# Six shared weight products of a mixture-of-experts loop cut from 160 to 128 tokens, with the tokens beyond 128 done in the two larger bodies

## The chip, the core and the metric

The kernel runs on one core of one Trainium2 chip. The metric is the device time of one execution in microseconds (us). Inputs, weights and output are float32.

## The reference, cut to what matters

The program is one decoder block over 1024 tokens of width 1024: a mixer (a short convolution and a recurrence over chunks) and then a mixture of experts, in which the change lies. Each token goes to 4 of 32 experts. For the tokens of one expert the reference computes

```python
h = xb @ gu_w[e] + gu_b[e]                      # 1024 -> 2048: gate and up, interleaved
x_glu = jnp.minimum(h[:, 0::2], SWIGLU_LIMIT)
x_lin = jnp.clip(h[:, 1::2], -SWIGLU_LIMIT, SWIGLU_LIMIT)
act = x_glu * jax.nn.sigmoid(SWIGLU_ALPHA * x_glu) * (x_lin + 1.0)
return act @ dn_w[e] + dn_b[e]                  # 1024 -> 1024
```

and adds each result, times its gate, into the row of its token. Which tokens an expert has is known only on the chip, so each expert's number of tokens is a value that the engines read and branch on.

## The kernel before, in words

**Order of the program.** TensorE runs the input projections, the recurrence, the output projection with the router, and then the expert loop. The expert loop is a loop on each engine over 33 turns; turn 0 only prepares expert 0. One turn of TensorE (`expert_pe`) consists of:

1. `down_half(n, 0)`: the first half of the down projection of expert n (8 products, 512 columns wide);
2. `transpose_tokens`: the transposes of the next expert's tokens;
3. `down_rest(n)` if expert n has more than 128 tokens (32 products with 32 columns of weights each), otherwise one small product;
4. `down_half(n, 1)`: the second half;
5. one of three copies of `gate_up` for the next expert, chosen by a branch on its size: 128, 144 or 160 tokens (`SIZES`);
6. `gate_up_end`, code that all three sizes share.

**The gate and up products.** `gate_up` has the weights as the stationary operand (128 by 128) and the tokens `xT` as the moving one (128, 144 or 160 wide). For each of 8 tiles f it makes 8 products for the gate half (k = 0) and 8 for the up half (k = 1), which accumulate over kt in PSUM: `ps[:, f % 2, 0:160]` for the gate, `ps[:, f % 2, 160:320]` for the up (`C` is 160). That would be 128 products; of the last eight (f = 7, k = 1) the body makes only kt = 0 and 1 (`SHARED = 6`), so that a body has 122. The remaining six, kt = 2 to 7, are in `gate_up_end` (L1856), which all sizes run and which is therefore 160 wide whatever the size.

**Who waits for them.** After each tile f the semaphore `s_gu` is raised (for the last tile by `gate_up_end`). VectorE and ScalarE then make the activation from the PSUM bank (`glu`, L1306 to L1313, always 160 wide) and write `actT[:, f, :]`. `down_half(n, 0)` waits before its first product for `actT` up to f = 6, and before its last for f = 7. The queue of SyncE (L506) reloads the weight slots: slot 3, which the six products read, is reloaded for the next expert once `s_gu` says that the last tile is done.

**Records.** A float32 product is seen in the trace as two weight loads (on PEld) and two matmul records (on PE): the 122 products of a body are 244 matmul records and 244 weight loads, the six products of L1856 are 12 and 12. The loop's code for TensorE is aligned to a block of 256 instructions (`pe.addr_align(FETCH_BLOCK, ...)`).

Of the kernel before, what the change touches and what calls it, by code (L numbers as in the profile page):

```python
# [13 lines left out]
P = 128  # L14
T = 1024
D = 1024
KT = D // P
# [12 lines left out]
C = 160  # L30
# [85 lines left out]
def build(nc, x, w_in_t, prm_d, lora_d, wgate_d, normw_d, w_out, router_w, router_b, gub_d, gu_w, dn_w,  # L116
          dn_b, consts_d, list0_d, entry_d, out, conv_d, bonus_d, xn_d, acc_d, list_d):
    ctx = ExitStack()
    with ctx:
# [8 lines left out]
        def at(kb, *shape):  # L128

            n = math.prod(shape)  # L130
            o = int(kb * 256)
            v = arena[:, o:o + n]
            if len(shape) == 2:
                v = v.rearrange("p (a b) -> p a b", b=shape[1])
            elif len(shape) == 3:
                v = v.rearrange("p (a b c) -> p a b c", b=shape[1], c=shape[2])
            elif len(shape) == 4:
                v = v.rearrange("p (a b c d) -> p a b c d", b=shape[1], c=shape[2], d=shape[3])
            return v

        ps = ctx.enter_context(nc.psum_tensor("ps", [P, 8, HALF], FP))
# [91 lines left out]
        wslot = [at(o, KT, HALF) for o in (0, 16, 32, 64, 80, 96)]  # L233
        xg = at(48, D)
        xg2 = at(52, PW)
        xT = at(136, KT, C)
# [106 lines left out]
        SHARED = 6  # L343
# [1060 lines left out]
        def _(pe):  # L1404
# [381 lines left out]
            for t in range(TT + 2):  # L1786
# [12 lines left out]
                if 0 <= u < TT:  # L1799
                    pe.wait_ge(s_xn2, u + 1)  # L1800
                    for g in range(2):
                        if u:
                            pe.wait_ge(s_t2c, 2 * u + g - 1)
                        for k in range(4):
                            kt = 4 * g + k
                            last = nc.tensor.transpose(ps[:, 4 + g, k * P:(k + 1) * P], xn2[u % 2][:, kt * P:(kt + 1) * P],
                                                       ident)
# [5 lines left out]
                if 0 <= u < TT:  # L1813
# [7 lines left out]
                    for kt in range(KT):  # L1821
                        g = kt % (P // E)
                        last = nc.tensor.matmul(ps[g * E:(g + 1) * E, 6, 0:P], rw[:, kt, :], xn2T[u % 2][:, kt, :],
                                                start=kt < P // E, stop=kt >= KT - P // E, skip_group_check=True)
# [9 lines left out]
            def gate_up(n, m, size):  # L1834

                for f in range(KT):
                    u = f // 2
                    if f % 2 == 0:
                        pe.wait_ge(s_wt[u], 16 * n + 16)
                    if f >= 2:  # L1840
                        pe.wait_ge(s_gd, 8 * n + KT + f - 1)
                    for k in range(2):
                        for kt in range(KT - SHARED if f == KT - 1 and k else KT):
                            if f == 0 and k == 0 and kt in (0, 4):
                                pe.wait_ge(s_xe, 3 * m + (2 if kt == 0 and size == P else 3))
                            o = (f % 2 * 2 + k) * P
                            last = nc.tensor.matmul(ps[:, f % 2, k * C:k * C + size],  # L1847
                                                    wslot[u][:, kt, o:o + P], xT[:, kt, 0:size],
                                                    start=kt == 0, stop=kt == KT - 1, skip_group_check=f == KT - 1)
                    if f < KT - 1:  # L1850
                        last.then_inc(s_gu, 1)

            def gate_up_end():

                for kt in range(KT - SHARED, KT):
                    last = nc.tensor.matmul(ps[:, 1, C:2 * C], wslot[3][:, kt, 3 * P:4 * P], xT[:, kt, :],  # L1856
                                            start=False, stop=kt == KT - 1, skip_group_check=True)
                last.then_inc(s_gu, 1)

# [35 lines left out]
            def expert_pe(r):  # L1895
# [4 lines left out]
                with pe.Fori(0, E + 1) as turn:  # L1900
                    n, m = r * E + turn - 1, r * (E + 1) + turn
                    with pe.If(turn > 0):
                        down_half(n, 0)
                    size = size_at(turn)
                    transpose_tokens(m)
                    with pe.If(size > 1):
                        down_rest(n)
                    with pe.If(size == 1):
                        pe.wait_ge(s_ye, 3 * n + 5)
                        nc.tensor.matmul(ps[0:REST, 6, 0:REST], actT[:, 0, P:C], ident[:, 0:REST], start=True, stop=True  # L1910
                                         ).then_inc(s_dn, 1)
                    with pe.If(turn > 0):
                        down_half(n, 1)
                    pe.wait_ge(s_sz, 2)
                    need = size_at(turn + 1)
                    with pe.If(need == 3):
                        gate_up(n + 1, m + 1, SIZES[2])
                    with pe.Else():
                        with pe.If(need == 2):
                            gate_up(n + 1, m + 1, SIZES[1])  # L1920
                        with pe.Else():
                            with pe.If(need == 1):
                                gate_up(n + 1, m + 1, SIZES[0])
                    with pe.If(need > 0):
                        gate_up_end()
# [62 lines left out]
```

## Time and profile before

| | |
|---|---|
| median of 3 runs | 2351.17 us (2351.09 to 2353.74) |
| profiled execution | 2356.62 us, its span 2355.1 us |
| mean granted TensorE clock | 0.99 |
| TensorE busy | 2296.2 us (98%) |
| weight loads busy | 1702.4 us (72%) |
| VectorE, ScalarE, GpSimd busy | 757.2, 483.4, 343.6 us |
| the chain that ended last, TensorE's share | 93% |

The profile has for each engine the records of its instructions, with start and duration. A matmul's record is longer than the time it takes from its neighbours, because matmuls overlap in the pipeline: what a record costs is the distance between starts, which the views give as the length of a stretch over its number of records. "The chain that ended last" is followed back from the last instruction, at each step to what released it or to the instruction before it on its engine; its pieces don't overlap, so a piece's length over its count is that distance. "issue" is time in which nothing that the profile shows was waited for.

### The profile page before, as it was taken

Reading aid. Unit: us, or ns where it says so; the run is one execution under the profiler, and the core shown is the slowest. Engines: PE = TensorE matmul, PEld = TensorE weight load, DVE = VectorE, ACT = ScalarE, POOL = GpSimd, SP = SyncE. Lnnn points to the kernel's source line nnn. Section 1 sums busy time; section 2 is a strip of 40 time slices with the busy share of each in tenths; the row PEclk is TensorE's granted clock in tenths of the full one; section 3 lists DMA queues with packets and bytes.
Section 4 is the critical chain, followed back from the end, with each engine's and each line's share of the span. In section 5 each row is a group of like instructions: output and inputs, shape, how many; then the busy total and the mean of one; then the engine's idle time right before and its main releaser. Section 6 shows DMA issues by size and latency. Waiting matters only on the chain.

```text
span 2355.1 us, 46545 instructions
## 1 busy us (share of the span) xinstructions
PE 2296.2 (98%) x18398; PEld 1702.4 (72%) x18399; DVE 757.2 (32%) x1802; ACT 483.4 (21%) x1008; POOL 343.6 (15%) x360
## 2 busy tenths in 40 slices
PE   7999999899999999999999999999999999999997
PEld 5443444799834578887888788877887788778876
DVE  2466511345333422322222222222222232222324
ACT  3323200244423301111111111111111111111113
POOL 0000000121102302111211121111111121112112
PEclk9999999999999899999999999999999999999998
DMA  3121111322352457986797779777797699768977
GB/s 120 36 70 36 49 59 62 93 76 71 105 239 100 142 223 279 335 349 263 295 339 308 282 276 337 286 303 300 295 348 305 254 335 353 285 245 326 346 305 256
DMA packets 111393, 534.97 MB, mean 227 GB/s; under 512 B 26755, under 2 KB 60695, under 8 KB 86736
## 3 DMA queue, kind: packets, MB, share of 16 engines
q1 hardware_dynamic: 89184, 489.30, 53.4%
q0 software_dynamic: 22160, 44.98, 7.6%
q8 instruction: 35, 0.57, 0.1%
q14 instruction: 14, 0.11, 0.0%
HBM read 485.24 MB, written 40.05 MB: 223 GB/s over the span
## 4 chain that ended last, share of the span: by engine, by line
PE 93%; DVE 3%; DMA 2%; issue 1%; ACT 1%; POOL 0%; SPq 0%; POOLq 0%; DVEq 0%; another core or an unknown queue 0%; ACTq 0%
PE ps L1847 38%; PE ps L1867 18%; PE ps L1409 13%; PE ps L1759 5%; PE ps L1877 2%; PE ps L1856 2%; PE ps L1554 2%; PE ps L1566 2%; PE ps L1560 1%; PE ps L1886 1%; DVE arena L1092 1%; PE ps L1440 1%; PE ps L1536 1%; DMA idx_g<-list_s 1%; PE ps L1655 0%
## 5 line engine op out<-in xcount | busy, mean ns | idle before, releaser
L1847 PEld LDWEIGHTS ps<-arena 128*128 128x128 f32 x7808 | 927.6, 191 | 17.5 <-issue 15.0
L1847 PE MATMUL ps<-arena 128*128 128x128 f32 (+2 forms) x7808 | 928.5, 282 | 2.3 <-ACT arena L937 2.3
L1867 PE MATMUL ps<-arena 128*128 128x512 f32 x1024 | 454.5, 597 | 0.0
L1409 PE MATMUL ps<-arena 128*128 128x512 f32 x832 | 361.1, 593 | 0.8 <-ACT arena L741 0.8
L1867 PEld LDWEIGHTS ps<-arena 128*128 128x128 f32 x1024 | 190.7, 190 | 222.1 <-issue 221.2
L1409 PEld LDWEIGHTS ps<-arena 128*128 128x128 f32 x832 | 157.2, 190 | 201.4 <-issue 201.4
L1306 DVE TENSOR_SCALAR arena<-ps,arena 128x160 f32<-128x160 f32 x256 | 98.3, 384 | 616.9 <-PE ps L1847 537.6
L942 ACT ACTIVATE arena<-arena 128x160 f32<-128x160 f32 x256 | 86.1, 336 | 825.2 <-DVE arena L1306 825.2
L644 POOL DMA_INDIRECT sum_s<-arena,idx_s x31 | 51.5, 1661 | 825.1 <-ACT arena L957 825.1
L1759 PE MATMUL ps<-arena 128*128 128x512 f32 x256 | 114.6, 602 | 1.5 <-DVE arena L1208 1.5
L1310 DVE SCALAR_TENSOR_TENSOR arena<-arena 128x160 f32<-128x160 f32 x256 | 83.3, 325 | 49.9 <-ACT arena L942 49.9
L1307 DVE TENSOR_SCALAR arena<-ps,arena 128x160 f32<-128x160 f32 x256 | 96.1, 376 | 0.0
L628 POOL DMA_INDIRECT arena<-xn_s,idx_g x33 | 36.5, 1105 | 391.9 <-issue 202.3
L1759 PEld LDWEIGHTS ps<-arena 128*128 128x128 f32 x256 | 48.3, 193 | 58.9 <-issue 58.9
L1327 DVE TENSOR_TENSOR arena<-ps,arena 128x512 f32<-128x512 f32 x31 | 21.4, 692 | 205.4 <-PE ps L1867 205.4
L1313 DVE TENSOR_TENSOR arena<-arena 128x160 f32<-128x160 f32 x256 | 83.3, 325 | 8.8
L934 ACT COPY arena<-ps 128x512 f32<-128x512 f32 x66 | 35.5, 588 | 213.2 <-PE ps L1886 212.0
L1323 DVE TENSOR_TENSOR arena<-ps,arena 128x512 f32<-128x512 f32 x31 | 21.4, 692 | 162.8 <-PE ps L1867 162.8
L957 ACT ACTIVATE arena<-arena,idx_s 128x512 f32<-128x512 f32 x31 | 22.4, 722 | 202.1 <-DVE arena L1327 202.1
L1856 PE MATMUL ps<-arena 128*128 128x160 f32 x384 | 58.1, 301 | 2.5 <-issue 2.5
L1856 PEld LDWEIGHTS ps<-arena 128*128 128x128 f32 x384 | 53.7, 191 | 2.7 <-issue 2.7
L1877 PE MATMUL ps<-arena 128*32 128x256 f32 x960 | 54.9, 380 | 0.0
(259 smaller groups left out, 1824.0 us busy)
## 6 DMA issues: line engine op xcount, KB each, us to landing
arena<-gu_w SPq DMA_DIRECT2D x128, 2048.0 KB, 13.4
arena<-dn_w SPq DMA_DIRECT2D x64, 2048.0 KB, 14.3
arena<-dn_b SPq DMA_DIRECT2D x32, 512.0 KB, 16.2
arena<-w_in_t SPq DMA_DIRECT2D x26, 512.0 KB, 3.2
arena<-arena SPq DMA_DIRECT2D x50, 256.0 KB, 2.7
arena<-x SPq DMA_DIRECT2D x4, 1024.0 KB, 8.3
arena<-w_out SPq DMA_DIRECT2D x2, 2048.0 KB, 10.7
arena<-x SPq DMA_DIRECT2D x8, 512.0 KB, 5.4
```

Source lines behind the costliest of these rows:

```text
L644: pool.indirect_dma_start(acc_d, bass.IndirectOffsetOnAxis(ap=idx_s[:, 0:1], axis=0), Yt, None, compute_op=ALU.add).then_inc(s_sc, 16)
L942: nc.scalar.activation(sgm[f % 2], gt[f % 2], ACT.Sigmoid, scale=ALPHA).then_inc(s_gs, 1)
L1306: nc.vector.tensor_scalar(gt[b], ps[:, b, 0:C], g0, LIMIT, ALU.add, ALU.min).then_inc(s_g1, 1)
L1307: nc.vector.tensor_scalar(lt[b], ps[:, b, C:2 * C], g1, LIMIT + 1, ALU.add, ALU.min).then_inc(s_gd, 1)
L1310: nc.vector.scalar_tensor_tensor(out=lt[b], in0=lt[b], scalar=1 - LIMIT, in1=sgm[b], op0=ALU.max, op1=ALU.mult).then_inc(s_l1, 1)
L1313: nc.vector.tensor_tensor(actT[:, f, :], lt[b], gt[b], ALU.mult).then_inc(s_act, 1)
L1409: last = nc.tensor.matmul(ps[:, bank + h, :], win[:, slot, kt * P:(kt + 1) * P], xnT[:, kt, h * HALF:(h + 1) * HALF], start=kt == 0, stop= ...
L1759: last = nc.tensor.matmul(ps[:, 2 * (t % 2) + h, :], mixT[:, k, t * P:(t + 1) * P], wo[:, k % RT, h * HALF:(h + 1) * HALF], start=k == 0, ...
L1847: last = nc.tensor.matmul(ps[:, f % 2, k * C:k * C + size], wslot[u][:, kt, o:o + P], xT[:, kt, 0:size], start=kt == 0, stop=kt == KT - 1, ...
L1856: last = nc.tensor.matmul(ps[:, 1, C:2 * C], wslot[3][:, kt, 3 * P:4 * P], xT[:, kt, :], start=False, stop=kt == KT - 1, skip_group_check= ...
L1867: last = nc.tensor.matmul(ps[:, 2 + h, :], actT[:, ft, 0:P], wslot[4 + h][:, ft, :], start=ft == 0, stop=ft == KT - 1)
L1877: last = nc.tensor.matmul(ps[g * REST:(g + 1) * REST, 6, 0:PW], actT[:, ft, P:C], wslot[4 + g // 2][:, ft, g % 2 * PW:(g % 2 + 1) * PW], s ...
```

## The change

The six products that all sizes share now cover 128 tokens (columns C to C + 128 of the bank), and each of the two larger bodies (144 and 160 tokens) ends with six products of its own, with the same stationary weights, over the 16 or 32 tokens beyond 128. `size` is a Python number, so that the 128-token body's code is unchanged. The same change is in the copy of the loop for further rounds, which isn't run with these inputs.

```diff
                     if f < KT - 1:
                         last.then_inc(s_gu, 1)
+                if size > P:
+                    for kt in range(KT - SHARED, KT):
+                        nc.tensor.matmul(ps[:, 1, C + P:C + size], wslot[3][:, kt, 3 * P:4 * P], xT[:, kt, P:size],
+                                         start=False, stop=kt == KT - 1, skip_group_check=True)
 
             def gate_up_end():
 
                 for kt in range(KT - SHARED, KT):
-                    last = nc.tensor.matmul(ps[:, 1, C:2 * C], wslot[3][:, kt, 3 * P:4 * P], xT[:, kt, :],
+                    last = nc.tensor.matmul(ps[:, 1, C:C + P], wslot[3][:, kt, 3 * P:4 * P], xT[:, kt, 0:P],
                                             start=False, stop=kt == KT - 1, skip_group_check=True)
                 last.then_inc(s_gu, 1)
```

## Rows read from the trace of the kernel before

**Rows 1.** The page: engines' busy time, and the chain's shares by line.
```profile
PE 2296.2 (98%) x18398; PEld 1702.4 (72%) x18399; DVE 757.2 (32%) x1802; ACT 483.4 (21%) x1008; POOL 343.6 (15%) x360
...
PE ps L1847 38%; PE ps L1867 18%; PE ps L1409 13%; PE ps L1759 5%; PE ps L1877 2%; PE ps L1856 2%; PE ps L1554 2%; PE ps L1566 2%; PE ps L1560 1%; PE ps L1886 1%; DVE arena L1092 1%; PE ps L1440 1%; PE ps L1536 1%; DMA idx_g<-list_s 1%; PE ps L1655 0%
```

**Rows 2.** Busy time of each engine in stretches of the expert loop.
```profile
core 0: us, PE busy (x) PEld busy (x) DVE busy (x) ACT busy (x) POOL busy (x), PEclk, DMA share, GB/s
...
822.00:857.00 35.00, 34.80 (x244) 34.80 (x244) 9.28 (x28) 3.79 (x9) 6.73 (x8) 0.95 0.89 338
...
860.00:869.00 9.00, 9.00 (x26) 5.07 (x26) 1.33 (x4) 0.34 (x1) 0.00 (x0) 0.81 0.63 231
...
935.00:2324.00 1389.00, 1389.00 (x9760) 1138.80 (x9759) 370.71 (x1044) 213.61 (x451) 242.73 (x240) 1.00 0.81 308
```

**Rows 3.** The chain that ended last: start, us, what; four stretches of it.
```profile
1450.68 33.14 PE ps L1847 x244
1483.83 1.63 PE ps L1856 x12
1485.46 6.87 PE ps L1867 x16
...
1504.07 29.89 PE ps L1847 x244
1533.96 1.63 PE ps L1856 x12
1535.59 6.87 PE ps L1867 x16
...
2069.34 29.89 PE ps L1847 x244
...
2119.47 27.24 PE ps L1847 x244
2146.71 1.63 PE ps L1856 x12
2148.35 6.87 PE ps L1867 x16
```

**Rows 4.** TensorE's groups by line and form: count, busy us, mean ns.
```profile
L1847 PE MATMUL ps<-arena 128*128 128x128 f32 x4148 | 466.2, 275 | 0.0
...
L1847 PE MATMUL ps<-arena 128*128 128x144 f32 x2928 | 360.6, 286 | 0.0
...
L1847 PE MATMUL ps<-arena 128*128 128x160 f32 x732 | 101.7, 302 | 2.3 <-ACT arena L937 2.3
L1856 PE MATMUL ps<-arena 128*128 128x160 f32 x384 | 58.1, 301 | 2.5 <-issue 2.5
```

**Rows 5.** Timeline of TensorE's matmuls in the token lists: start, us, line, form, count.
```profile
796.68 2.37 PE L1782 MATMUL ps<-cst,arena 128*128 128x1 f32 x20
```

**Rows 6.** The line L1782: duration of its records, min/median/max in ns.
```profile
L1782 PEld LDWEIGHTS ps<-cst,arena x32: 192/192/333, 796.7 to 809.9; 128*128 128x128 f32 x32
L1782 PE MATMUL ps<-cst,arena x32: 250/250/372, 796.7 to 810.0; 128*128 128x1 f32 x32
```

**Rows 7.** The chain in the router stage, with 32-wide products.
```profile
716.05 0.34 PE ps L1776 x2
716.39 0.22 PE ps L1777 x2
...
723.56 0.14 PE ps L1770 x2
```

**Rows 8.** The chain, turn 0 and the start of turn 1.
```profile
822.20 35.09 PE ps L1847 x244
857.29 2.46 issue
859.75 2.43 PE ps L1856 x12
862.17 8.02 PE ps L1867 x16
```

**Rows 9.** The DMA queues, 852 to 870 us: packets, MB, share of 16 engines.
```profile
q8 instruction: 2, 0.03, 0.7%
```

**Rows 10.** The DMA queues, 1000 to 2340 us: the whole list.
```profile
## 3 DMA queue, kind: packets, MB, share of 16 engines
q1 hardware_dynamic: 35155, 375.56, 70.1%
q0 software_dynamic: 17472, 33.80, 10.6%
issues: line engine op xcount, KB each, median us to landing
```

**Rows 11.** Timeline of VectorE and TensorE around L1856 in a 128-token turn.
```profile
2278.08 0.33 DVE L1313 TENSOR_TENSOR arena<-arena 128x160 f32<-128x160 f32 x1
2278.78 1.80 PE L1856 MATMUL ps<-arena 128*128 128x160 f32 x12
2280.41 4.03 PE L1867 MATMUL ps<-arena 128*128 128x512 f32 x9
...
2281.94 0.33 DVE L1313 TENSOR_TENSOR arena<-arena 128x160 f32<-128x160 f32 x1
```

**Rows 12.** Waits of SyncE's queue, 880 to 2290 us.
```profile
SPq L506 <- PE ps L1856: 217.2, 30, 8.2
```

**Rows 13.** The chain at its end.
```profile
2288.72 7.08 PE ps L1867 x16
2295.82 0.70 DVE arena L1327
...
2301.72 12.42 DMA idx_g<-list_s
```

## The prediction

> **What bounds the kernel now.** I read the page first: TensorE is busy for 98% of the span, and lines of TensorE make up 93% of the chain that ended last, the gate and up bodies (L1847) alone 38% and the shared end L1856 2% [rows 1]. A share of busy time can mislead, so I then read the stretches of the expert loop: from 935 to 2324 us TensorE was busy for all of 1389.00 us, at a granted clock of 1.00 (2.4 GHz), while VectorE, ScalarE and GpSimd had 371, 214 and 243 us and the DMA engines 0.81 of the time [rows 2]. Last the chain itself: in a turn of each size, body, shared end and down projection follow each other with no gap (1483.83 + 1.63 = 1485.46, and so in the others) [rows 3]. So in the loop nothing counts but the distance between the starts of TensorE's records. Whatever a product costs there is paid in full, and whatever is saved is gained in full.
>
> **What sets that distance.** A body is 244 matmul records. The reader is to divide each body's length by 244 [rows 3]: 33.14 us is 135.8 ns a record at 160 wide, 29.89 us is 122.5 ns at 144, 27.24 us is 111.6 ns at 128. From 160 to 144 the distance falls by 13.3 ns, which is two cycles of 2.4 GHz for each of the 16 columns (32 / 2.4 = 13.3); from 144 to 128 it falls by only 10.9. At 128 wide something else has begun to bind. What it is can be read off products that have hardly any columns: L1782 has 128 by 128 stationary operands, each loaded anew, and a moving operand one column wide. Twenty of its records lie in 2.37 us [rows 5]; less the last one's 250 ns [rows 6] that leaves 2.12 us for 19 distances, 111.6 ns each. That is the distance of the 128-wide records to the digit, with 1 column in place of 128. So the load of the next weights sets a floor of 111.6 ns a record, and at 128 columns or fewer the columns are free. The narrowing therefore gains only the part above the floor, and a product of 16 or 32 columns costs as much as one of 128.
>
> **The sizes.** By form there are 4148, 2928 and 732 records of 128, 144 and 160 wide [rows 4]; over 244 these are 17, 12 and 3 experts, 32 in all. L1856 has 384 records, 12 for each expert, as it should.
>
> **Part 1, the shared end, 160 to 128 wide.** Twelve records take 1.63 us now (135.8 ns each) [rows 3], and 12 x 111.6 = 1.34 us after: 0.29 us less for each expert. Two of the 32 need a word. The last expert's end lies behind the point at which the chain leaves TensorE for the last time (2295.82 us) [rows 13]; it counts for nothing. The first one's end comes after a wait of 2.46 us for instructions, with a clock that is granted at 0.81 on average in that stretch [rows 2, 8]; it took 2.43 us, and in proportion to its columns would fall by 0.49. Against this, the records queued ahead of that wait will be shorter (below), so that I count it at 0.29 as well. 31 x 0.29 = 9.0 us less.
>
> **Part 2, six products more in the larger bodies.** Six products are 12 records with a weight load each, which all lie on TensorE's path since nothing else does. 12 x 111.6 ns = 1.34 us, for 12 + 3 = 15 experts: 20.1 us more. All 15 lie before the chain leaves TensorE; the last body 144 wide starts at 2069.34 [rows 3]. The trace has no 16-wide product with these weights, so this price must be bounded. Above: a record 16 or 32 wide can't well cost more than one 144 wide in the same place, 122.5 ns, or 22.1 us in all. Below: records with 32 moving columns in the router stage stand in the chain as two in 0.22 us, two in 0.34 and two in 0.14 [rows 7]. The last is 70 ns each, but only because the first of the two has its weights loaded behind a 512-wide record; 0.22 us, in the midst of narrow ones, is 110 ns. In the new place the record before the first narrow one is 144 or 160 wide, and hides no more of a load than it does now. 70 ns would be 12.6 us in all. I take 111.6, the row of twenty in sequence, which is nearest in everything but the width (1 where 16 and 32 are wanted, and 128 gives the same).
>
> There is a rule that speaks for a much lower price. The Trainium skill, in "TensorEngine Tiling (Array Packing)", section Performance Considerations, says that a matmul has some 60 cycles of overhead and that one of a single column takes as long as one of 60. By it alone the twelve records would be 12 x 60 / 2.4 = 300 ns, an estimate from that page, and the change would gain 4.5 us (180 records at 25 ns, less 9.0). "TensorE: Matmul & The Clock Gate", section LDWEIGHTS, gives a weight load 128 columns over 1.2 GHz, 107 ns, and there the trace agrees nearly (111.6 measured).
>
> **Part 3, the rest, at nothing.** The shared end is now over 0.29 us sooner after the body of a 128-token expert. `down_half` waits for the activation of tile 6 before its first product: VectorE ends it at 2278.41, and L1867 starts at 2280.41 [rows 11], so 2.0 us of cover become 1.7. The activation of tile 7 ends at 2282.27, 1.9 us after that start, and its product is the last of eight that take 6.87 us: 4 us of cover stay. If the first cover were gone, each 0.1 us missing would cost 17 x 0.1 = 1.7 us. In the larger bodies both covers grow. SyncE's queue stands at L506 and waits for L1856 in 30 turns, 217.2 us in all [rows 12]: it waits for TensorE and not the other way. Weight slot 3 is asked for 1.05 us later in the larger turns and 0.29 earlier in the small ones, and with the DMA engines at 0.81 no transfer comes to limit TensorE. VectorE reads the same 160 columns as before.
>
> **The sum.** -9.0 + 20.1 = +11.1 us. A 128-token turn becomes 0.29 us shorter, a larger one 1.05 us longer. Against the profiled execution, 2356.62 us with a span of 2355.1, this gives 2367.7. That execution was 5.4 us above the median of the runs (2351.17); the same 11.1 us on the median gives 2362.3 us, 0.47% more.
>
> **The rivals.** About 0.2%, 4.7 us, is what a measurement of this kernel can tell from no change.
>
> *A. Narrow products are nearly free.* If a record of 16 or 32 columns cost its columns or a small fixed time, and its weight load lay hidden, the change would be faster. The point from which the sign turns is where 180 records cost the 9.0 us saved: 50 ns a record. At 25 ns it is 4.5 - 9.0 = -4.5, or 2346.7 us; at nothing, 2342.2 us. Against it are the twenty records of L1782 [rows 5], which have the least columns possible and yet stand 111.6 ns apart. For it is only the 0.14 us for two behind a wide record [rows 7]; at that 70 ns the sum is 12.6 - 9.0 = +3.6, 2354.8 us, within the band, as is all between 24 and 76 ns.
>
> *B. The code no longer stays on the chip.* The larger bodies get 24 instructions each, 12 loads and 12 matmuls. The cost of a jump to code that isn't there is in the trace: 2.46 us in turn 0, then L1856 at 2.43 in place of 1.63 and L1867 at 8.02 in place of 6.87 at the lower clock, 4.4 us together [rows 3, 8], with two transfers of instructions near it [rows 9]; from 1000 to 2340 us the list of queues has none [rows 10]. So all that the loop runs stays resident. If the 48 instructions ended that, with one such stall in each turn with a larger body, it would be 15 x 4.4 = 66 us: about 2428 us. Per turn's distinct code I count from the records 3 x 488 for the bodies, 24 for the shared end, 64 + 128 for the down projection, 24 for the transposes and the small product: 1704, and 1752 after, without waits and branches. "Runtime: NRT & Kernel Launch", section Instruction fetch mechanics, gives TensorE room for 2048 instructions; by that page the loop fits before and after.
>
> *C. The one stall shifts.* The code behind the larger bodies moves by 24 and 48 instructions. The wait of turn 0 may vanish (-4.4: 2357.9 us), or one more may show in the first turns (+4.4: 2366.7 us). The records ahead of the jump become shorter as well, 12 x 24 ns = 0.3 us less cover, so that a small lengthening is likelier than not; it is in the 0.2 us that I gave up in part 1.
>
> *D. The change does nothing to the pace of the shared end*, because 128-wide products there stay at 135.8. The bodies of 128 tokens, with the same weights' form, speak against it. It would be +20.1, 2371.3 us.
>
> **How the numbers follow.** The forecast, 2362.3 with its own range from 2360.5 to 2364 (a price of 107 to 116 ns for a narrow record gives -0.8 and +0.8, the rest is the scatter of a median), has 0.80. C has 0.09, on both sides alike. B has 0.03, D 0.02. A has 0.01 below 24 ns and 0.05 in the band. The range takes in the forecast and C: 2357.5 to 2367. Faster by over 0.2% is A's first part, 0.01; within the band A's second, 0.05; slower 0.94.
>
> **What would show it.** Right: L1847's records 16 wide (144 in number) and 32 wide (36) in the larger bodies, each six products 1.34 us in the chain; L1856 128 wide with 1.34 us for 12 records; larger turns 1.05 us longer, the 128-token turns 0.29 us shorter; no waits of TensorE inside the loop after the first turns. Wrong: narrow records less than 111 ns apart, L1856 still near 1.6 us, an "issue" piece after a body in turns beyond the first, or transfers of instructions after 1000 us. What would make the prediction wrong is above all the price of a narrow record, since one number multiplied by 180 carries the sign.

## The result, and the profile after

The changed kernel takes 2478.45 us (2476.5 to 2484.24, 5 runs) against 2353.74 us for the kernel before (2351.09 to 2354.28, 5 runs): 1.0535 times, 95% interval 1.0522 to 1.0548. The forecast was 2362.3, with a range up to 2367. The profiled execution took 2484.24 us, its span is 2482.7 us. 125 us came in place of 11.

The page of the changed kernel, engines and the chain's shares, as [rows 1]; the body is still L1847, the narrow products are L1854, the shared end is now L1860 and the wide down projection L1871:

```profile
PE 2346.9 (95%) x18578; PEld 1730.3 (70%) x18579; DVE 757.3 (31%) x1802; ACT 483.3 (19%) x1008; POOL 343.4 (14%) x360
...
q8 instruction: 96, 1.57, 0.3%
...
PE 90%; issue 4%; DVE 3%; DMA 1%; ACT 1%; POOL 0%; SPq 0%; POOLq 0%; DVEq 0%; ACTq 0%
```

TensorE's share fell from 98 to 95%, and "issue", waiting for nothing that the profile shows, makes 4% of the chain. The queue that brings instructions moved 96 packets, against 35 in the kernel before. From 1000 us to the end of the loop, where the kernel before has none [rows 10], the changed one has 64 of them:

```profile
q8 instruction: 64, 1.05, 0.3%
```

TensorE's waits in the changed kernel (line that waited, releaser: us in total, times, longest):

```profile
PE ps L1860 <- issue: 42.6, 16, 4.6
PE ps L1871 <- issue: 37.2, 7, 5.6
PE ps L1440 <- DVE arena L1030: 11.8, 1, 11.8
```

The chain, a 144-token turn whose predecessor was 144 wide as well (start, us, what), then the 128-token turn that follows it:

```profile
1085.49 29.89 PE ps L1847 x244
1115.38 1.24 PE ps L1854 x12
1116.62 1.43 PE ps L1860 x12
...
1136.67 27.24 PE ps L1847 x244
1163.92 1.35 PE ps L1860 x12
...
1166.96 3.72 issue
1170.68 10.13 PE ps L1871 x16
```

The first turn is as forecast: 24 records of narrow and shared products in 2.67 us, 111 ns each, and no gap. In the second the body is as before, the shared end takes the forecast 1.35 us, and then TensorE stands still for 5.41 us (1165.27 to 1170.68): the chain leaves it for VectorE and ScalarE, whose activations had been hidden before, and 3.72 us of waiting remain. The 16 records behind it take 10.13 us in place of 6.87 [rows 3]; the granted clock shows why. Stretches of the changed kernel, columns as in [rows 2]:

```profile
1136.00:1163.00 27.00, 27.00 (x240) 26.68 (x239) 9.63 (x28) 4.36 (x9) 8.05 (x8) 1.00 0.95 347
1171.00:1182.00 11.00, 11.00 (x28) 5.01 (x27) 0.69 (x1) 0.71 (x2) 0.00 (x0) 0.74 0.39 161
```

After the standstill the clock is granted at 0.74 on average, so in part at 1.2 GHz.

In a 144-token turn behind a 128-token one the standstills lie elsewhere:

```profile
1025.49 29.89 PE ps L1847 x244
1055.38 1.24 PE ps L1854 x12
1056.62 4.62 issue
1061.24 1.43 PE ps L1860 x5
1062.67 1.77 issue
1064.44 1.65 PE ps L1860 x7
1066.10 7.64 PE ps L1871 x16
```

One wait stands ahead of the shared end and one between its 5th and 6th record. In this code there is nothing to wait for between two of these products. In all eight turns in which the shared end is interrupted it is after 5 records. So the engine's code is late. That the place of the second wait is an edge between two blocks of code is worked out in the next section.

Compared turn by turn (start of one body to the start of the next), turns 0 to 30 are 128.1 us longer together, for a span 127.6 us longer:

| turns | number | longer by, each |
|---|---|---|
| 144 or 160 tokens, not in the next row | 7 | 1.05 us |
| 144 tokens, the expert before being 128 or 160 | 7 | 8.90 to 11.30 us, 69.4 together |
| 128 tokens, not in the next row | 9 | -0.29 us (one -0.52) |
| 128 tokens, the expert before being 144 | 7 | 7.02 to 8.40 us, 52.8 together |
| turn of expert 0 | 1 | 1.40 us |

The products alone make 15 x 1.05 - 16 x 0.29 = 11.1 us of this. The 14 turns of the second and the fourth row carry the remaining 117 us. TensorE stands idle in them for 75.8 us ahead of L1860 and L1871 (the 79.8 of the list above, less 4.0 in turn 0), and for none in the kernel before. The other 41 us are products behind a wait that take longer, like the 10.13 us in place of 6.87. A change of size alone is not enough: a 128-token turn behind a 160 and a 160 behind a 128 lost nothing.

The packets of instructions lie in the same turns. First the 128-token turn above, 1136.5 to 1189 us, then a 144-token turn behind a 128, 1232.8 to 1292 us:

```profile
q8 instruction: 5, 0.08, 0.7%
...
q8 instruction: 3, 0.05, 0.4%
```

In the repeated 144-token turn, 1085 to 1136 us, there is none. From turn 4 on each of the 14 turns that lose time has three to five such packets, each other turn none to two.

### The profile page after: what moved, and what is told of

Read it like the earlier page. It is cut to its first block, busy times and chain, and to the rows that moved or that the text cites. A ratio compares the mean times of both kernels' runs of the same rounds, so it can differ in the third digit from the quotient of the medians.

```text
span 2482.7 us, 46905 instructions
## 1 busy us (share of the span) xinstructions
PE 2346.9 (95%) x18578; PEld 1730.3 (70%) x18579; DVE 757.3 (31%) x1802; ACT 483.3 (19%) x1008; POOL 343.4 (14%) x360
## 4 chain that ended last, share of the span: by engine, by line
PE 90%; issue 4%; DVE 3%; DMA 1%; ACT 1%; POOL 0%; SPq 0%; POOLq 0%; DVEq 0%; ACTq 0%
PE ps L1847 36%; PE ps L1871 19%; PE ps L1409 13%; PE ps L1759 5%; PE ps L1860 2%; PE ps L1881 2%; PE ps L1554 2%; PE ps L1566 2%; PE ps L1560 1%; PE ps L1890 1%; DVE arena L1092 1%; PE ps L1854 1%; PE ps L1536 1%; PE ps L1440 1%; DMA idx_g<-list_s 0%
## 5 line engine op out<-in xcount | busy, mean ns | idle before, releaser
L1847 PEld LDWEIGHTS ps<-arena 128*128 128x128 f32 x7808 | 925.9, 191 | 17.8 <-issue 16.2
L1847 PE MATMUL ps<-arena 128*128 128x128 f32 (+2 forms) x7808 | 927.1, 281 | 2.3 <-ACT arena L937 1.4
L1871 PE MATMUL ps<-arena 128*128 128x512 f32 x1024 | 482.7, 627 | 37.5 <-issue 37.2
L1871 PEld LDWEIGHTS ps<-arena 128*128 128x128 f32 x1024 | 200.8, 202 | 278.1 <-issue 277.0
L1409 PE MATMUL ps<-arena 128*128 128x512 f32 x832 | 362.2, 595 | 0.8 <-ACT arena L741 0.8
L1759 PE MATMUL ps<-arena 128*128 128x512 f32 x256 | 115.8, 607 | 1.5 <-DVE arena L1208 1.5
L1860 PE MATMUL ps<-arena 128*128 128x128 f32 x384 | 60.1, 311 | 42.6 <-issue 42.6
L1860 PEld LDWEIGHTS ps<-arena 128*128 128x128 f32 x384 | 54.6, 221 | 44.0 <-issue 44.0
L1554 PE MATMUL ps<-arena 64*64 64x64 f32 x1328 | 54.9, 222 | 0.3
```

Of the source, the lines that this page charges most:

```text
L1409: last = nc.tensor.matmul(ps[:, bank + h, :], win[:, slot, kt * P:(kt + 1) * P], xnT[:, kt, h * HALF:(h + 1) * HALF], start=kt == 0, stop= ...
L1554: last = nc.tensor.matmul(out_at(s, 0, h, r), MTs[s][own(h), r, :], Tst[s][own(h), r, :], start=True, stop=True)
L1759: last = nc.tensor.matmul(ps[:, 2 * (t % 2) + h, :], mixT[:, k, t * P:(t + 1) * P], wo[:, k % RT, h * HALF:(h + 1) * HALF], start=k == 0, ...
L1847: last = nc.tensor.matmul(ps[:, f % 2, k * C:k * C + size], wslot[u][:, kt, o:o + P], xT[:, kt, 0:size], start=kt == 0, stop=kt == KT - 1, ...
L1860: last = nc.tensor.matmul(ps[:, 1, C:C + P], wslot[3][:, kt, 3 * P:4 * P], xT[:, kt, 0:P], start=False, stop=kt == KT - 1, skip_group_chec ...
L1871: last = nc.tensor.matmul(ps[:, 2 + h, :], actT[:, ft, 0:P], wslot[4 + h][:, ft, :], start=ft == 0, stop=ft == KT - 1)
```

## The experiments

What to look for is the code's place. In the compiled program, counted from the loop's head, a product is 4 instructions, and the loop has 1758 instructions before the change and 1806 after it. Its head stands one instruction into a block of 256. So the edge between the seventh and the eighth block, 1792, falls just behind the fifth matmul of L1860, where the trace has its gap; before, the loop ended ahead of this edge.

**The head of the loop moved within its block, nothing else.**

```diff
-            pe.addr_align(FETCH_BLOCK, offset=1, max_nops=0)
+            pe.addr_align(FETCH_BLOCK, offset=33, max_nops=0)
```

with 33, 35, 37, 41 and 49: 32, 34, 36, 40 and 48 instructions further. For 32:

> The kernel before, with the head of the expert loop placed 32 instructions further into its block of 256 (offset 33 in place of 1); nothing is added or changed. In the compiled program the loop has 1758 instructions before the change and 1806 after it, and 7 blocks hold 1792. Theory (the loop's code must end within its seventh block): it ends at 1790 or 1791, so no stall comes: 2351 to 2356 us. Rival 1 (the length of the code counts, not its place): no stall either, the same time. Rival 2 (the narrow products themselves bring the stalls): the same time.

For 34:

> The kernel before, with the loop's head 34 instructions further into its block, two more than in the other run; nothing is added or changed. Theory (seven blocks): the loop's last instruction, the branch back, now lies in the eighth block, so each change between the 128-token body and a larger one brings waits for instructions, 7 to 11 us in each of 14 turns: 2440 to 2490 us, and about 60 more transfers of instructions. Rival 1 (length, not place): 2351 to 2356 us. Rival 2 (the narrow products): 2351 to 2356 us. Rival 3 (what hurts is that the shared end is split between two blocks, not that the loop reaches into one more): the shared end lies whole in the seventh block here, so 2351 to 2356 us.

Measured: 1.0006 times before (0.9996 to 1.0017) and 1.0008 (0.9998 to 1.0019). Neither stalls. My first theory had drawn the line at the edge of the eighth block itself, and it fell with the second run: the branch back lies in the eighth block there, and nothing happens.

**The same length without the work.**

```diff
+                    with pe.If(need > 3):
+                        for _ in range(48):
+                            pe.sem_inc(s_pe_apart, 1)
```

> The kernel before, with 48 semaphore instructions behind a branch at the end of the loop that is never taken, so that the loop's code is as long as after the change and the work of TensorE is that of before. Theory (seven blocks): 2440 to 2490 us, with waits in the turns in which the body changes. Rival 1 (length): slow as well. Rival 2 (the narrow products): 2351 to 2356 us. Rival 3 (a split shared end): 2351 to 2356 us.

1.0002 times before (0.9991 to 1.0012). This run tells nothing. `need` was declared to be at most 3, so the branch was dropped when the program was compiled, and what ran was the kernel before. I noticed it only after the next runs; the expectation of the run at 48 leans on it wrongly.

**The same work in less code.** The narrow products are written once, 32 wide, behind a branch that both larger sizes take.

```diff
+                    with pe.If(need > 1):
+                        gate_up_beyond()
                     with pe.If(need > 0):
                         gate_up_end()
```

> The kernel after, with the narrow products written once, 32 wide, behind a branch that both larger sizes take, in place of a copy in each body: TensorE runs as many products as after the change, and the loop is 1783 instructions long. Theory (seven blocks): it fits, so nothing is left but the products' own price, -9.0 and +20.1 us as the prediction had it: 2360 to 2365 us, 1.0047 times before. Rival 2 (the narrow products bring the stalls): 2470 to 2485 us. Rival 1 (length, with some threshold between 1758 and 1806): either.

2363.08 us, 1.0046 times before (1.0029 to 1.0063). In the trace every larger turn is 1.05 us longer than before, every 128-token turn but one 0.29 us shorter, and no wait for instructions stands in the loop behind turn 0. So the products cost what the prediction said, and the other 115 us are not theirs.

**The head 48 and 40 further.**

> The kernel before, with the loop's head 48 instructions further into its block (offset 49). Nothing is added, and the shared end and the loop's last instruction have the places that they have after the change, about 14 instructions into the eighth block. The theory as first put (the loop's code must end within its seventh block) has fallen, since neither two instructions over the edge nor 48 that are never run brought a stall. Theory 2 (what counts is that TensorE's queue runs some way through the eighth block, so that the block behind it is fetched as well, which is one more than stays resident): slow, 2440 to 2490 us, some 60 more transfers of instructions, stalls in 14 turns. Rival A (the place of the bodies: after the change the branch to the two smaller ones lands 4 instructions ahead of a block's edge, here it doesn't): 2351 to 2356 us. Rival B (the narrow products): ruled out by the run with one copy of them.

> The kernel before, with the loop's head 40 instructions further (offset 41): the shared end's last 6 or so instructions and the branch back lie in the eighth block. Theory 2: between the two ends that are known, 2 instructions (no stall) and 14 (stalls, if the other run shows it); if entering the block in sequence is enough it is slow, 2440 to 2490 us, if it takes more than 8 instructions it is 2351 to 2356 us. Rival A (place of the bodies): 2351 to 2356 us.

Measured: 1.0889 (1.0869 to 1.0909) and 1.1028 times (1.1008 to 1.1048). Waits of TensorE, 48 further:

```profile
PE ps L1867 <- issue: 78.3, 16, 5.6
PE ps L1856 <- issue: 42.2, 16, 4.1
PE ps L1847 <- issue: 19.3, 8, 2.6
```

Not one instruction is added here, no product is narrower, and the kernel loses 210 and 243 us. The gap inside the shared end stands after 5 records at 48, as after the change, and after 9 at 40, where the edge has moved 8 instructions, that is 4 matmuls with their loads. The bodies lie elsewhere than after the change, and now 128-token turns that follow each other stall as well: 16 and 17 waits stand ahead of L1867 in place of 7, and so more than 125 us are lost. Why just these turns, I can't say.

**Where the line lies.**

> The kernel before with the loop's head 36 instructions further (offset 37): the last one or two instructions of the shared end and the two branches behind it lie in the eighth block. Known so far: head 34 further brings no stall (only the branch back in the eighth block), 40 further does. Theory 2 (TensorE's queue has to run some way through the eighth block): nearer to 34 than to 40 in what runs there, so the outcome tells where the edge is; if a product in the eighth block is enough, 2440 to 2600 us, if it takes several, 2351 to 2356 us. Rival 3 (a shared end split between two blocks): slow.

2357.11 us, 1.0010 times (0.9999 to 1.0022), no stall behind turn 0. The shared end's last product reaches into the eighth block, so that a shared end split between two blocks is not enough either. With the head 36 further the loop's last instruction is the third of the eighth block, with 40 further the seventh. The line is between.

**Padding that stays in the program.** The bound of `need` is declared one higher, so that the branch can't be dropped; 64 instructions ahead of the shared end, or 48 behind it.

> The kernel before, with 64 semaphore instructions between the bodies and the shared end, behind a branch that no size takes (the sizes' declared bound is 4 in place of 3, so that the branch stays in the program; the earlier run with a padding was compiled to the kernel before itself, because its bound made the branch superfluous, and told nothing). The shared end now lies whole in the eighth block. Theory 2: slow, 2440 to 2600 us. Rival 3 (a split shared end is what hurts): 2351 to 2356 us. Rival 1 (length of code that is run): 2351 to 2356 us.

> The same kind of padding, 48 instructions that never run, behind the shared end: the shared end lies whole in the seventh block as before, and only the branch back lies in the eighth, about 16 instructions into it. Theory 2 in the form that counts what runs there: no stall, 2351 to 2356 us. In the form that counts how far into the block the branch back lies: slow, 2440 to 2600 us.

With the 64: 2672.51 us, 1.1347 times (1.1310 to 1.1384). With the 48: 2655.11 and 2728.96 us in two executions, for which there is no ratio; the shorter one is 302 us above the kernel before. Waits with the 48 behind:

```profile
PE ps L1867 <- issue: 108.4, 21, 8.3
PE ps L1847 <- issue: 51.5, 20, 3.8
PE ps L1856 <- issue: 42.7, 11, 4.3
```

In the second one the shared end lies whole in the seventh block, as before the change, and only an addition and the branch back run in the eighth, some 15 instructions into it. It is slow all the same, where three instructions that ran at the start of the block cost nothing. So it isn't how much runs there; what remains is how far in the loop's end lies. One difference is left open: here the eighth block is entered by a jump over the padding, and no run jumps to its first instructions turn after turn. My expectation named both forms, by what runs there and by how far in it lies; the second held.

**One body less.** Sizes 128 and 160 alone (`SIZES = [P, C]`, and the branch for the third size gone): once with the head 40 further, once with 561 instructions that never run in the place of the missing body, which put the shared end and the branch back exactly where the slow kernel with 64 of padding has them.

> Sizes 128 and 160 alone, so that the loop has one body less (1261 instructions, in 5 blocks), and the head 40 instructions further, so that its shared end is split over the edge between the fifth and the sixth block and the branch back lies 20 instructions beyond. The 12 experts of 129 to 144 tokens run the 160-wide body: 12 x (33.14 - 29.89) = 39 us more than before. Theory 2 (one block more than stays resident): there is room for a sixth block and the one behind it, so no stall: 2388 to 2395 us, no waits for instructions after the first turns. Rival 3 (any edge crossed by the shared end or just ahead of the branch back): stalls as with the head 40 further in the loop of three bodies, 100 to 240 us on top.

> Sizes 128 and 160 alone (one body less), and in the place of the missing body 561 instructions behind a branch that is never taken, so that the shared end and the branch back have the very places in the eighth block that they have in the kernel with 64 instructions of padding, which lost 300 us. The 12 experts of 129 to 144 tokens run the 160-wide body, 39 us more. Theory 2a (what counts is how many blocks the loop really touches, with the one behind the last): two of the eight blocks are never entered, so all that is touched stays resident: 2388 to 2398 us, no waits for instructions after the first turns. Theory 2b (what counts is the stretch from the loop's head to its end): stalls in nearly all turns with a change of body and in most others, 2550 to 2720 us.

2398.04 us, 1.0181 times (1.0152 to 1.0211), and 2396.35 us, 1.0189 times (1.0158 to 1.0219). The medians lie 44.5 and 43.5 us above the kernel before, where the 12 wider bodies make 39. Of the rest, turn 0 has 1.6 and 5.0 us in the profiled executions; what remains I put down to the spread of two runs each. Waits of the second:

```profile
PE ps L1440 <- DVE arena L1030: 11.7, 1, 11.7
PE ps L1856 <- issue: 7.8, 1, 7.8
PE ps L1429 <- ACT arena L763: 7.2, 3, 2.4
```

One wait for instructions ahead of the shared end, in turn 0, and none behind. From 1010 to 2330 us neither kernel brings an instruction, where the one with 64 of padding has

```profile
q8 instruction: 164, 2.69, 1.0%
```

So a shared end across an edge does no harm, a loop end deep in the eighth block does no harm, and a loop that spans eight blocks does no harm, as long as two of them are never entered. What harms, as far as these runs go, is the number of blocks that the turns between them touch.

**A version that uses this.** The 128-token body does its last six products itself and skips the shared end, which stays 160 wide for the two larger sizes. That is 24 instructions more, and the loop ends at 1782, within the seventh block.

```diff
-                        for kt in range(KT - SHARED if f == KT - 1 and k else KT):
+                        for kt in range(KT - SHARED if f == KT - 1 and k and size > P else KT):
...
-                    if f < KT - 1:
+                    if f < KT - 1 or size == P:
...
-                    with pe.If(need > 0):
+                    with pe.If(need > 1):
                         gate_up_end()
```

> A candidate: the 128-token body does its last six products itself, 128 wide, and the shared end stays 160 wide and is run by the two larger sizes alone; the larger turns are those of before. The loop has 1782 instructions, which end within the seventh block. All theories of the stall: no stall. Twelve records at 111.6 in place of 135.8 ns in 16 of the 17 turns of 128 tokens that count: 4.6 us less than before, 0.998 times.

2346.75 us, 0.9974 times before (0.9963 to 0.9984), faster than both kernels. The chain of a 128-token turn in it:

```profile
2111.38 28.59 PE ps L1847 x256
2139.96 6.87 PE ps L1867 x16
```

256 records in 28.59 us are 111.7 ns each. The turns say 0.29 us less for each 128-token expert (0.52 in one) and nothing for the larger ones, 4.9 us where 4.6 was expected. A further 3.0 us of the profiled execution are in turn 0. Its wait for instructions is not shorter (2.79 us, before 2.46); its products ran at a higher clock: the body took 33.41 us in place of 35.09 (granted clock 1.00 and 0.95), L1867 6.87 in place of 8.02. I don't count these 3 us as an effect of the edit.

## Why the prediction was wrong, by its own steps

**The distance of narrow records, right.** The trace after has the very forms, and they cost what L1782 cost [rows 5, 6]:

```profile
L1854 PE MATMUL ps<-arena x180: 179/263/276, 855.6 to 2221.1; 128*128 128x16 f32 x144, 128*128 128x32 f32 x36
```

144 and 36 records as counted, 12 in 1.24 us and the 12 behind them in 1.43, 2.67 together against 2 x 1.34. By that the trace goes against the 60 cycles of the Trainium skill's "TensorEngine Tiling (Array Packing)", section Performance Considerations, for a product whose weights are loaded anew: 300 ns for twelve would be less than a quarter of what they took.

**Parts 1 and 2 and their sum, right.** +1.05 and -0.29 us a turn, 11.1 us in all, are in the undisturbed turns of the changed kernel and in every turn of the kernel with one copy, which came out at 2363.08 against 2362.3.

**Part 3, at nothing, right in the undisturbed turns** (no wait of TensorE for VectorE or a transfer there), and beside the point in the others.

**Rival B is what happened, and it had 0.03.** The step that failed is the sentence "by that page the loop fits before and after", by which waits for instructions inside the loop entered the sum at nothing; they and what followed them made 117 us. Three things were wrong in it. I compared a count without waits and branches (1704 and 1752; really 1758 and 1806) with room for 2048 instructions, and took what remained for a margin. I took all code of the loop to be what must be held, and the runs show another sum: whole blocks of 256 that are touched, with an eighth block into which this loop may reach by three instructions and not by seven. And I didn't look at where in its blocks the code lies, though [rows 10] had the sign that everything was held and the kernel aligns its loop to a block.

**What held the ninth block.** The Trainium skill, "Runtime: NRT & Kernel Launch", section Instruction fetch mechanics, says that TensorE's room is 128 KiB, refilled in blocks of 256 instructions, which makes eight of them, and that the sequencer fetches the next block while it works through the current one. Eight blocks of the loop and one behind them are nine. The sizes agree: 64 packets in the loop carry 1.05 MB, 16.4 KB each, an eighth of the room. The runs agree too: three instructions into the eighth block nothing happens, seven or more and blocks are fetched in turn after turn; with two blocks never entered it stops. That the ninth block is the one behind the loop was only argued; no view shows which block a transfer brings.

**The price of a stall, too low.** Rival B used turn 0, 4.4 us with its lower clock, once in each turn with a larger body, 66 us. It was 117 us over 14 turns, 8.4 each: two or more blocks are late one after the other (4.62 and 1.77 us above), and the turns that pay are those with a 144-token body behind another size or a 128 behind a 144, so 128-token turns are among them. A 144-token turn behind a 144 fetched nothing from turn 4 on. 2428 us would still have been too low by 50.

**Rivals A and D** are refuted by L1854's and L1860's records. C was small as said: in the profiled executions of the kernels with three bodies turn 0 lies between 3.0 us below and 2.6 us above that of the kernel before.

## What to carry to other kernels

Where a loop's code nearly fills the instruction store, code has a price by its place: before adding any, count the compiled instructions of the loop from a block's start, in whole blocks. Blocks that no turn enters can be left out, but instructions that never run still push what lies behind them further, as the 48 and 64 of padding did. A queue of instruction packets that is silent through a long loop says that all of it is held, and not how much more there is room for. To narrow a float32 product with weights of its own below 128 columns gained nothing here (111.6 ns a record at 128 and at 1), and to split one into two costs one whole load more.

## What the runs showed that I had not expected

A kernel lost 210 to 243 us, 9 to 10%, by nothing but the place of its loop, 40 or 48 instructions further into a block; with 36 it lost none that could be measured. Two instructions in the eighth block, behind 48 that never ran, cost over 300 us, more than a shared end split in two. And a loop with an even later end lost nothing where two blocks between were never entered.
